# Two pairs of weight columns as plain block products instead of one, and nine places for the token tiles, in a one-core streaming encoder kernel

## What is computed

```python
h = rmsnorm(x, norm_g)                       # (tokens, 2048)
proj = einsum('btd,dc->btc', h, w_in)        # 2048 -> 10240 columns
xa, za, v, bg, cg, zb, ga, gb = split(proj)
ya = pool_mixer(xa, state_pool, ...) * silu(za)
yb = bg * conv_mixer(cg * v, state_conv, ...) * silu(zb)
merged = sigmoid(ga + b) * (ya @ w_proj_pool) + sigmoid(gb + b) * (yb @ w_proj_conv)
y = rmsnorm(x + merged @ w_out, final_norm_g)   # and the new states
```

## Time and profile before

| | |
|---|---|
| median of 3 runs | 2533.45 us (2532.53 to 2534.23) |
| the profiled execution's own time | 2525.83 us |
| its span, first to last instruction | 2524.0 us |
| TensorE busy | 2453.2 us, 97% of the span |
| VectorE busy | 1589.7 us, 63% |
| ScalarE busy | 885.4 us, 35% |
| GpSimd busy | 105.4 us, 4% |
| moved by DMA | 409.80 MB, mean 162 GB/s |
| granted TensorE clock | 0.995 of full speed in the mean |

### The profile page before, as it was taken

The page is one execution under the profiler, slowest core; times in us unless marked ns, Lnnn a source line. Parts: engine busy times, 40 slices in busy tenths (PEclk is TensorE's granted clock), DMA queues, the critical chain, the costliest instruction groups (busy, mean ns, idle before and its releaser), DMA issues.

```text
span 2524.0 us, 44735 instructions
## 1 busy us (share of the span) xinstructions
PE 2453.2 (97%) x18762; PEld 2441.9 (97%) x18762; DVE 1589.7 (63%) x2299; ACT 885.4 (35%) x1486; POOL 105.4 (4%) x208
## 2 busy tenths in 40 slices
PE   6999999999999999999999999999999999999997
PEld 5999999999999999999999999999999998999997
DVE  6655444444444476777867877755755878678764
ACT  5333333333333343333322222233533434354454
POOL 1000000000000000000000000000000011000000
PEclk9999999999999999999999999999999999999999
DMA  6344333333333453434343233445547667466795
GB/s 220 114 172 173 102 102 104 104 104 104 104 104 104 139 196 135 153 133 161 132 148 136 102 134 134 152 157 190 196 156 269 234 238 264 143 224 230 252 293 181
DMA packets 217517, 409.80 MB, mean 162 GB/s; under 512 B 9379, under 2 KB 171891, under 8 KB 200102
## 3 DMA queue, kind: packets, MB, share of 16 engines
q1 hardware_dynamic: 194342, 276.70, 33.0%
q0 software_dynamic: 22464, 126.57, 13.5%
q10 hardware_dynamic: 512, 3.67, 0.4%
HBM read 277.72 MB, written 129.18 MB: 161 GB/s over the span
## 4 chain that ended last, share of the span: by engine, by line
PE 88%; DVE 5%; DMA 3%; issue 2%; ACT 1%; POOL 0%; DVEq 0%; ACTq 0%; SPq 0%; POOLq 0%
PE ps L883 84%; PE ps L1040 2%; DVE ops L1356 1%; PE ps L964 1%; DVE lo L1301 1%; DMA opm_raw<-opq 1%; DMA raw<-in_w_out_dram 1%; DVE opm L1356 1%; DMA xn<-in_x_prompt_dram 1%; DVE ops L1371 0%; DMA ops_raw<-opq 0%; DVE sb L1320 0%; PE ps L983 0%; ACT hi L1061 0%; DVE pb L1350 0%
## 5 line engine op out<-in xcount | busy, mean ns | idle before, releaser
L883 PE MATMUL ps<-ops,hi 128*128 128x272 f32 x10768 | 1471.2, 289 | 18.9 <-DVE pb L1350 6.6
L883 PEld LDWEIGHTS ps<-ops,hi 128*128 128x128 f32 x10768 | 1402.3, 188 | 21.9 <-DVE pb L1350 7.8
L883 PE MATMUL ps<-ops,lo 128*128 128x272 f32 x5384 | 784.9, 288 | 0.0
L883 PEld LDWEIGHTS ps<-ops,lo 128*128 128x128 f32 x5384 | 717.2, 188 | 0.0
L1350 DVE TENSOR_TENSOR pb<-pb,ps 128x544 f32<-128x544 f32 x426 | 306.6, 720 | 382.4 <-PE ps L883 382.1
L1061 ACT ACTIVATE hi<-sb 128x512 fp32r<-128x512 f32 x444 | 280.8, 632 | 635.0 <-PE ps L883 576.9
L1301 DVE TENSOR_TENSOR lo<-raw,hi 128x512 fp32r<-128x512 f32 x401 | 276.0, 689 | 279.2 <-ACT hi L1061 276.9
L1301 DVE TENSOR_TENSOR lo<-sb,hi 128x512 fp32r<-128x512 f32 x444 | 304.9, 687 | 191.4 <-ACT hi L1061 190.2
L1061 ACT ACTIVATE hi<-raw 128x512 fp32r<-128x512 f32 x401 | 253.1, 632 | 472.5 <-PE ps L883 422.4
L1080 ACT COPY pb<-ps 128x544 f32<-128x544 f32 x216 | 132.3, 612 | 408.3 <-PE ps L883 408.3
L883 PE MATMUL ps<-opm,hi 128*128 128x384 f32 x896 | 177.7, 338 | 13.8 <-DVE pbm L1350 7.6
(11 more groups left out here) (130 smaller groups left out, 1028.8 us busy)
## 6 DMA issues: line engine op xcount, KB each, us to landing
raw<-in_w_in_dram SPq DMA_DIRECT2D x160, 512.0 KB, 4.0
pb<-part SPq DMA_DIRECT2D x39, 1088.0 KB, 6.5
part<-pb POOLq DMA_DIRECT2D x37, 1088.0 KB, 5.0
raw<-in_w_out_dram SPq DMA_DIRECT2D x64, 512.0 KB, 5.4
gates<-pb POOLq DMA_DIRECT2D x16, 1088.0 KB, 9.1
gate<-gates SPq DMA_DIRECT2D x32, 544.0 KB, 7.1
ops_raw<-opq SPq DMA_DIRECT2D x15, 1088.0 KB, 9.3
opq<-ts POOLq DMA_DIRECT2D x12, 1088.0 KB, 5.5
```

The lines of the kernel that those rows point to most:

```text
L883: mm = nc.tensor.matmul(ps[b][:, c, 0:n], w[:, w_slot, kt * P:(kt + 1) * P], operand[:, kt, half, k * n:(k + 1) * n], start=fresh and kt = ...
```

## The change

1. `NC = 2`: pairs 0 and 1 are both done as eight plain products. Pair 1 has eight products instead of seven, and no sums of weights or tokens are needed before pair 2. The drains of both plain pairs are on ScalarE.
2. The eight plain products of a pair use PSUM places 0 and 1 alone; place 3 stays with the transposes.
3. Nine places for the token tiles, so no load waits for a transpose. Tiles 0 and 1 are loaded in two halves of 1024 columns each, one on SyncE's queue and one on ScalarE's; tiles 3, 5, 7 whole on SyncE's queue, 2, 4, 6, 8 whole on ScalarE's. Weights follow on SyncE's.
4. The small rows (`g_rows`, `vec_rows`, `state_rows`) are loaded by GpSimd's queue, after its constants.
5. The orders of transposes, copies and roundings are rewritten, and ScalarE makes two of the eighteen copies of transposed tokens, in eight instructions each.

```diff
-    SLOT0 = NQ - 4
+    NC = 2
+    SLOT0 = NC * NQ - 4 * NC
...
-            if g == 0:
-                k = (0, 1, 0, 3)[s - SLOT0]
+            if g < NC:
+                k = (s - SLOT0) % 2
...
-        TURNS = [(t, a) for t in range(EARLY) for a in range(2)] + [(t, 0) for t in range(EARLY, TT)]
-        TURNS += [(t, 1) for t in (6, 7, 5, 8)]
+        TURNS = ((0, 0), (0, 1), (1, 0), (1, 1), (2, 0), (3, 0), (4, 0), (2, 1), (3, 1), (5, 0), (6, 0), (4, 1),
+                 (7, 0), (8, 0), (5, 1), (6, 1), (7, 1), (8, 1))
...
-            def load_tokens(t):
-                if t >= 4:
-                    sp.wait_ge(x_turned, TURNED[t - 4, 1])
-                sp.dma_start(xn[t % 4][0:rows(t), :], x_rows(t)).then_inc(x_landed[t], 16)
...
+            for t in (0, 1):
+                sp.dma_start(xn[t][:, 0:D // 2], x_rows(t)[:, 0:D // 2]).then_inc(x_landed[t], 16)
+            for t in (3, 5):
+                sp.dma_start(xn[t][:, :], x_rows(t)).then_inc(x_landed[t], 16)
             load_weights(0)
+            sp.dma_start(xn[7][:, :], x_rows(7)).then_inc(x_landed[7], 16)
+            for m in range(1, 2 * NC + 3):
+                load_weights(m)
...
-                if i == 4:
-                    wait_product_drained(pe, SLOT0)
-                if i == 5:
-                    pe.wait_ge(h_copied, len(TURNS))
+                if i in (4, 5):
+                    wait_product_drained(pe, SLOT0 + 4 * g + i - 4)
+                if i in (0, 1) and g > 0:
+                    wait_product_drained(pe, SLOT0 + 4 * g + i - 2)
...
+            for t in (0, 1):
+                act.dma_start(xn[t][:, D // 2:D], x_rows(t)[:, D // 2:D]).then_inc(x_landed[t], 16)
+            for t in range(2, TT, 2):
+                act.dma_start(xn[t][0:rows(t), :], x_rows(t)).then_inc(x_landed[t], 16)
```

More of the change, by code:

```diff
@@ L115, in bass_hybrid_stream_step @@
         g, q = divmod(s, NQ)
-        if g > 0 and (is_partial(g) or q not in ACT_Q):
+        if g >= NC and (is_partial(g) or q not in ACT_Q):
             nd += 1
@@ L206, in bass_hybrid_stream_step @@
         OP_B = KQ * 2 * TH * 4
-        xn = [at(f"xn{k}", (1 + k // 2 * 2) * OP_B + k % 2 * D * 4, [D]) for k in range(4)]
+        xn = [at(f"xn{t}", place * OP_B + t0 * D * 4, [D])
+              for t, (place, t0) in enumerate(((0, 0), (0, 1), (5, 0), (5, 1), (6, 0), (3, 0), (3, 1), (1, 0), (1, 1)))]
         h1raw = at("h1raw", 2 * OP_B, [3, KQ, TOK])
         assert 2 * D * 4 <= OP_B == KQ * TOK * 4
-        vec_rows = at("vec_rows", 6 * OP_B, [P])
-        state_rows = at("state_rows", 6 * OP_B + P * 4, [E])
-        g_rows = at("g_rows", 6 * OP_B + P * 4 + E * 4, [P])
+        vec_rows = at("vec_rows", 6 * OP_B + D * 4, [P])
+        state_rows = at("state_rows", 6 * OP_B + D * 4 + P * 4, [E])
+        g_rows = at("g_rows", 6 * OP_B + D * 4 + P * 4 + E * 4, [P])
         h0raw = at("h0raw", PB0, [KE, TOK])
@@ L491, in bass_hybrid_stream_step, with wait_copied @@
         NF = len(FIRST_OPS)
+        def wait_copied(eng, n):
+            k = sum(e in COPIED_ACT for e in TURNS[:n])
+            eng.wait_ge(h_copied_dve, n - k)
+            if k > 0:
+                eng.wait_ge(h_copied_act, k)
         stored_before = {}
@@ L790, in whole_pair @@
             def whole_pair(g):
-                for q in range(NQ):
-                    if q >= 3:
-                        wait_product_drained(pool, NQ * g + q)
+                if g < NC:
+                    wait_product_drained(pool, SLOT0 + 4 * g + 3)
+                for q in range(3, NQ) if g >= NC else ():
+                    wait_product_drained(pool, NQ * g + q)
             def store_pair(g):
@@ L837, in store_states @@
                     r += n
-            for s in range(NS):
+            for g in range(NC - 1):
+                store_pair(g)
+            for s in range(NC * NQ, NS):
                 g, q = divmod(s, NQ)
@@ L1000, in _ @@
             nc.tensor.transpose(flat[0][:, 0:KD], g_rows[0:KD, :], ident[0:KD, 0:KD]).then_inc(g_turned, 1)
-            for i in range(2 * EARLY):
+            for i in range(10):
                 if i == 4:
@@ L1004, in _ @@
                 turn(i)
[L1006 to L1011, removed]
-            for s in range(NQ, NS):
+            i = 10
+            for g in range(NC):
+                for k, turns in enumerate((0, 1, 1, 2, 2, 1, 1, 0) if g == 0 else (0,) * 8):
+                    for e in range(turns):
+                        turn(i)
+                        i += 1
+                    first_product(g, k)
+            for s in range(NC * NQ, NS):
                 g, q = divmod(s, NQ)
@@ L1066, in drain @@
                     return
-                if q == 0:
+                if q == 0 and g >= NC:
                     if g == FIRST[M0]:
@@ L1211, in scale, with copy_turned @@
                 r = rows(t)
-                own = xn[t % 4][0:r, :]
+                own = xn[t][0:r, :]
                 act.wait_ge(rstd_made, t + 1)
                 nc.scalar.activation(own, own, ACT.Copy, scale=rstd[0:r, t:t + 1]).then_inc(x_scaled_act, 1)
+            def copy_turned(t):
+                i = TURNS.index((t, 1))
+                r = rows(t)
+                act.wait_ge(x_turned, i + 1)
+                act.wait_ge(g_made, 1)
+                for k in range(KE):
+                    each = nc.scalar.activation(h1raw[:, 2 * (k % 2), k // 2, t * P:t * P + r],
+                                                flat[2 + i % 2][:, k * P:k * P + r], ACT.Copy,
+                                                scale=g_col[:, KE + k:KE + k + 1])
+                each.then_inc(h_copied_act, 1)
             for t in range(4):
@@ L1232, in _ @@
             split_hi(SLOT0 + 3)
+            drain(SLOT0)
             first_operand_hi(2)
-            drain(SLOT0)
+            drain(SLOT0 + 1)
+            copy_turned(5)
             first_operand_hi(3)
-            drain(SLOT0 + 1)
-            split_hi(NQ)
+            split_hi(SLOT0 + 4)
+            copy_turned(7)
+            split_hi(SLOT0 + 5)
+            drain(SLOT0 + 2)
+            split_hi(SLOT0 + 6)
             first_operand_hi(4)
-            split_hi(NQ + 1)
-            drain(SLOT0 + 2)
+            drain(SLOT0 + 3)
+            split_hi(SLOT0 + 7)
             first_operand_hi(5)
-            split_hi(NQ + 2)
-            for s in range(NQ, NS):
+            drain(SLOT0 + 4)
+            drain(SLOT0 + 5)
+            first_operand_hi(6)
+            split_hi(NC * NQ)
+            split_hi(NC * NQ + 1)
+            first_operand_hi(7)
+            drain(SLOT0 + 6)
+            split_hi(NC * NQ + 2)
+            for s in range(NC * NQ, NS):
                 g, q = divmod(s, NQ)
@@ L1248, in _ @@
                 split_hi(s + R - 1)
-                if g == 1 and q < 2:
-                    first_operand_hi(q + 6)
                 if ph == H1:
@@ L1624, in _ @@
             scale(7)
+            copy_turned(TURNS.index((4, 1)))
             copy_turned(TURNS.index((7, 0)))
```

180 lines of the change are left out of this document (91 added, 89 removed).

## The result

The changed kernel takes 2518.95 us in the median of 4 runs (2517.09 to 2520.93), the kernel before 2532.99 (2531.53 to 2534.23, 4 runs). The ratio is 0.995, with a 95% interval from 0.9939 to 0.9961, so it is 10 to 15 us faster.

The account below looks back on a forecast made before the run. TensorE, busy 97% of the span, was taken as the bound. Pair 2 starting at 91.9 instead of 101.43 gives 9.5 us; 2533.45 − 9.5 = 2524.0 us, with an 8-in-10 range of 2521.5 to 2529.5.

Parts of the forecast that it names:

- What decides: pair 2's start: Whole kernel: the gain is how much earlier than 101.43 us pair 2's first product starts; TensorE's work behind is unchanged.
- Eight plain products, 7.1 removed against 3.0 added: Pair 1: one more product costs 3.02 us; drain waits of 2.10 and 3.61 and half clock (at least 1.4) go.
- From the second product to pair 2: TensorE from 39.8 us: products 45.3, transposes 5.6, late low part 0.4, small waits 0.8; pair 2 starts at 91.9.
- The walk: Step-by-step timing of ScalarE's queue to the first product (34.7 us), then on to pair 2's start at 91.9.
- the arrival of tiles 2 and 3: Token loads at the beginning: both tiles arrive side by side at about 17.0 us, 16 if the weights' room is gained.
- The rival of the half columns: First loads: tiles 0 and 1 in 4 KB rows cost 5.1 us more, gain 4.4, time 2529.0; chance 0.15.
- The median of the runs is 7.62 above that execution: Last term of the sum: old kernel's median 2533.45 us against its profiled 2525.83, used to forecast the new median.
- The nine places bring little here.: Token loads before the first product: it starts at about 34.7 us against 35.38; ScalarE limits from tile 4 on.
- Half clock on the first product: First products: TensorE runs at half clock after waiting some 2 us, giving 2525.5 to 2527 us; chance 0.12.
- ScalarE's copies: Two half tiles on ScalarE: 2.4 us each; in a rival of chance 0.08, 5.0 each or late `h1raw` stores lose 2 to 4.
- ScalarE wasn't held by its issues: Rival at the beginning: six load issues hold ScalarE until about 25 to 27 us, time 2538; chance 0.04.
- the old two waits came back in pair 2: Rival in pair 2: pair 1's waits of 5.7 us return there with the extra product, net 2532, no change; chance 0.03.

## Why the prediction was right in sign and 5 us off

*What decides: pair 2's start.* Right. In each run the beginning moved and TensorE's work behind it stayed the same.

*Eight plain products, 7.1 removed against 3.0 added.* Right. Alone in the old order they brought 4.5 us between the first product and pair 2, for the 4.1 of the prediction. A product costs 3.02.

*From the second product to pair 2.* The walk had 39.8 to 91.9, which is 52.1. Measured are 38.02 to 90.09, which is 52.07. Products, transposes and the 0.4 for the late low part (0.42) stand. What is left over is 0.8, as much as I had put in for small waits, but that was a guess, and no idle time over a quarter of a us stands behind it.

*The first step that failed is the arrival of tiles 2 and 3, "both at about 17.0 (bounds: 16 if the weights' room is gained)".* They were there at 15.00 and before 17.10. I took the old arrival as a matter of bytes and kept the old rate, 227 GB/s in the first us. That rate belonged to the old form of the first loads, two halves of 64 rows. In halves of columns it is 374, with whole tiles 360, with halves of rows again 239. The bytes of the first 6 us at the old rate are 1.36 MB, at the new one 2.24. The diff showed that these loads changed their form, and I asked only whether the new form was slower. The rival of the half columns had the right place and the wrong sign, and the low end of the range had no case for a faster load. The price of the old form can be read from the run with halves of rows: third square at 19.41 and pair 2 at 94.8, so with it even the walk's 17.0 would have been too early. This step is worth 1.8 us of pair 2's start (90.09 against 91.9).

*The second is a term of the sum, "The median of the runs is 7.62 above that execution".* It measured 1.86 (2518.95 against the profiled 2517.09), 5.8 us less. The 7.62 came from one profiled execution, the fastest of its kernel; the three repeats, one of before and two of after, have 2.3, 3.3 and 1.4. Against it stand the part behind pair 2, which took 2.3 us more than in the sum, and 0.3 between span and own time. With the 1.8 from pair 2 these make the 5 us between 2524.0 and 2518.95.

*"The nine places bring little here."* Half right, and badly put. With the new loads, but without the plain pair, they bring nothing that can be measured (0.9998), and the plain pair in the new order without them brings nothing that can be measured either (0.9995). Together they bring 11. The new order of transposes needs more tiles at once, and waits 3.03 and 6.42 us where it doesn't have them. In the old order the plain pair gives 5.6 and keeps the wait of 2.40. So of the 11.3 us, 4.5 are the plain pair by itself. The other 6.8 came in no run but with places, new order and new loads together; they were counted in the walk, but not under that name. Of them 4.7 hang on the form of the first loads (94.8 against 90.1). How the rest divides isn't shown, since the plain pair with the nine places in the old order was not run.

*Scatter.* My range had nothing for the scatter of the part behind pair 2 and of the medians. The three timings of the same change gave 14.0, 10.5 and 9.3 us, 11.3 in the mean, which is what the profile says. By that mean the time beside 2532.99 would be 2521.7, just inside the range, so that it fell outside is in part chance; the 1.8 us are not. The part behind pair 2 took 2422.6 us in the first profile of before, 2425.4 in the second, and 2424.9, 2425.0 and 2426.2 in those of after. TensorE's idle time there stays within 1.1 us, so it goes with the clock and not with waits. What decides the clock there stays open.

*Rivals.* Half clock on the first product did come: its first 16 matmuls took 2.85 us instead of 2.18. It cost pair 2 nothing in this profile: the third profile has the first product at full clock and pair 2 at the same 90.1, because the second product waits for tile 6. With whole tiles the half clock lasted longer and did cost over a us. What this rival said of the beginning is a wrong reading: "the granted clock is 1.00 from 2 to 15 us with TensorE nearly idle". The column says so, but TensorE's own rows in the kernel before don't. Here are the transposes from 8 to 18 us, from 22 to 26 and from 26.2 to 34, with the mean ns of one at the end:

```profile
L942 PE MATMUL ps<-ident,xn 128*128 128x128 f32 x16 | 3.4, 401 | 3.1 <-DVE xn L1586 3.1
L942 PE MATMUL ps<-ident,xn 128*128 128x128 f32 x18 | 4.0, 417 | 0.0
L942 PE MATMUL ps<-ident,xn 128*128 128x128 f32 x37 | 4.8, 277 | 3.4 <-ACT xn L1214 2.4 <-DVE h0raw L1597 0.5 <-DVE h1raw L1599 0.4
```

The column has 1.00, 0.50 and 1.00 for the three. The first transposes run like those at 0.50, so TensorE did begin slow, and the 1.00 there is no evidence against it. It didn't move the sum, which is walked on ScalarE up to the first product.

ScalarE's copies took 2.18 per half tile (I had 2.4), and the rounding of T2 stood at 71.32. ScalarE wasn't held by its issues. But SyncE was, which I hadn't looked at:

```profile
3.86 13.15 SPq L549 DMA_DIRECT2D raw<-in_w_in_dram  x2
```

Two issues of weights took 13.15 us where one takes 0.45. The second of the two, from 4.37, took 12.65 by itself. So an issue can hold its engine for long; this one had no other work to hold up. `g_rows` landed after 5.4 us on GpSimd's queue, within the bound, and its transposition started at 8.16, in time:

```profile
g_rows<-in_norm_g_dram POOLq DMA_DIRECT2D x1, 8.0 KB, 5.4
```

The fixed 2.0 us that the Trainium skill states (DMA: Bandwidth & Descriptors, "Anatomy of one DMA") is less than half of what this load took; the row decides, and it was taken while the tiles were being loaded.

Two of the prediction's small sums don't come out. Operand 0 is rounded by 32.25, not 32.4, by its own 1.9. And if the old two waits came back in pair 2, with their half clock, 9.5 less 5.7 and 1.4 leaves 2.4, so 2531 and not 2532. Neither changes the forecast.

## What to carry to other kernels

When a change gives a load another shape, ask of the measured rate whether it belongs to the bytes or to the old shape, in both directions. Before calling a part worthless, ask what other part needs it: here the plain pair in the new order and the new loads in the old order each measured nothing, and made 11 us together. Where the effect is near the scatter, compare the start of the first stage that both programs share, and give the scatter of the rest its place in the range.

## What the runs showed of the hardware

- Where the first tiles came from HBM in halves of 64 of the 128 partitions, the DMA engines were busy (share 1.00 to 1.03) at 219 to 239 GB/s from 2 to 8 us. The same bytes over all partitions moved at 360 (rows of 8 KB) and 374 GB/s (rows of 4 KB) on the same two queues. No run here shows why; none took the partitions apart from the engines that serve them.
- SyncE stood 12.6 us on a single issue, that of its third weights, with 5.2 MB issued ahead of it on its queue, 1 MB of them weights in rows of 1 KB. With six tiles in halves it stood 10.3 us on the issue of tile 7, again behind 5.2 MB. ScalarE's queue took 4.7 MB of tokens in six issues of 0.6 us. Whether bytes or rows decide was not tried.
- With the same program, the same 40 us of the tail ran at a granted clock of 0.96 in one execution and 0.83 in another.
- The column of the granted clock read 1.00 from 8 to 18 us, while transposes took 401 ns each, as at 0.50 (417) and not as at 1.00 later (277).
- A wait can take back what an earlier start gave: with only the loads changed, the first product came 2 us earlier, and two 7 us stretches at 0.52 of the clock, where the kernel before had 0.76, came behind unchanged waits; pair 2 started at the same time.
